# Transposed first hidden columns in a spare accumulator bank, with a semaphore of their own

## The reference, cut to what matters

```python
for i in range(DEPTH_2):
    mix = ...                          # attention of the layer
    h = layer_norm(DEEPNORM_ALPHA * h + mix, ln_mix_g[i], ln_mix_b[i])
    h = layer_norm(DEEPNORM_ALPHA * h + sq_relu_mlp(h, mlp_w_in[i], mlp_w_out[i]),
                   ln_mlp_g[i], ln_mlp_b[i])
```

## Time and profile before

| what | value |
|---|---|
| median of three runs | 1334.9 us (1334.03 to 1336.12) |
| the profiled execution, its own time | 1336.56 us |
| its span, first to last instruction | 1334.8 us |
| mean granted clock of PE, share of full speed | 0.956 |
| PE busy | 1177.5 us, 88% of the span |
| DVE busy | 691.5 us, 52% |
| ACT busy | 490.5 us, 37% |

### The profile page before, as it was taken

One profiled execution on the slowest core, in us unless ns is written; L12 is line 12 of the kernel. 1 busy time (PEld: TensorE's weight loads), 2 busy tenths in 40 slices (PEclk: granted clock), 3 DMA queues, 4 the chain that ended last, 5 costly groups with the idle time before them and its releaser, 6 DMA issues.

```text
span 1334.8 us, 22156 instructions
## 1 busy us (share of the span) xinstructions
PE 1177.5 (88%) x9399; PEld 922.1 (69%) x9399; DVE 691.5 (52%) x1033; ACT 490.5 (37%) x709; POOL 3.9 (0%) x8
## 2 busy tenths in 40 slices
PE   6999999998885767657566999999999999999997
PEld 5688888886542434334233799778888899788886
DVE  4699867774220102011010666765666767766665
ACT  5653446553110100000000554644444456444442
POOL 0000000000000000000000000000000000000000
PEclk9999999999997878888788999999999999999999
DMA  9867487689999999999999955353636245463610
GB/s 358 309 216 261 170 308 268 252 342 406 425 426 426 429 427 427 426 430 428 428 429 415 305 201 190 126 190 130 248 131 247 82 159 218 147 227 134 246 69 32
DMA packets 92743, 369.94 MB, mean 277 GB/s; under 512 B 6654, under 2 KB 14636, under 8 KB 79604
## 3 DMA queue, kind: packets, MB, share of 16 engines
q1 hardware_dynamic: 92280, 367.92, 70.6%
q10 hardware_dynamic: 380, 0.81, 0.2%
HBM read 367.66 MB, written 1.05 MB: 276 GB/s over the span
## 4 chain that ended last, share of the span: by engine, by line
PE 71%; DMA 22%; DVE 3%; ACT 2%; issue 1%; SPq 1%; DVEq 0%; ACTq 0%
DMA arena<-in_moe_w 20%; PE ring L2222 8%; PE ring L2710 6%; PE ring L2211 5%; PE acc L2337 5%; PE acc L2339 5%; PE acc L2338 5%; PE ring L2224 4%; PE ring L2213 3%; DMA own<-in_moe_w 2%; PE acc L2195 2%; PE acc L2196 2%; PE acc L2197 2%; PE ring L2385 1%; PE ring L2387 1%; PE ring L2386 1%
## 5 line engine op out<-in xcount | busy, mean ns | idle before, releaser
L2710 PE MATMUL ring<-arena 128*32 128x256 f32 x1952 | 148.8, 470 | 73.5 <-DMA arena<-in_moe_w 72.5
L2710 PEld LDWEIGHTS ring<-arena 128*32 128x32 f32 x1952 | 76.7, 134 | 141.3 <-issue 76.0
L1430 DVE TENSOR_TENSOR wlo<-arena,whi 128x2048 fp32r<-128x2048 f32 x56 | 128.2, 2290 | 53.7 <-ACT whi L953 53.7
L1880 DVE TENSOR_TENSOR arena<-arena,ring 128x128 f32<-128x128 f32 x32 | 12.2, 380 | 256.0 <-ACT arena L1226 256.0
L1226 ACT ACTIVATE arena<-ring 128x128 f32<-128x128 f32 x32 | 8.9, 277 | 346.2 <-PE ring L2710 342.7
L953 ACT ACTIVATE whi<-arena 128x2048 fp32r<-128x2048 f32 x56 | 107.0, 1910 | 46.3 <-PE acc L2339 29.7
L2222 PE MATMUL ring<-xboth,whi 128*128 128x512 f32 x288 | 102.4, 398 | 0.0
L2224 PE MATMUL ring<-xboth,wlo 128*128 128x256 f32 x288 | 80.8, 281 | 0.0
L2337 PE MATMUL acc<-whi,hidhi 128*128 128x512 f32 x168 | 66.7, 397 | 2.9 <-DVE arena L2131 2.2
L2211 PE MATMUL ring<-hboth,w1hi 128*128 128x512 f32 x192 | 68.0, 399 | 0.1
L2748 PE MATMUL acc<-above 32*128 32x256 f32 x512 | 46.0, 425 | 24.4 <-DVE above L1887 16.6
(11 more groups left out here) (462 smaller groups left out, 2719.0 us busy)
## 6 DMA issues: line engine op xcount, KB each, us to landing
arena<-in_moe_w SPq DMA_DIRECT2D x75, 2048.0 KB, 22.2
arena<-in_mlp_w_in SPq DMA_DIRECT2D x16, 2048.0 KB, 9.7
arena<-in_mlp_w_out SPq DMA_DIRECT2D x16, 2048.0 KB, 8.0
own<-in_moe_w SPq DMA_DIRECT2D x14, 2048.0 KB, 25.7
arena<-in_w_in SPq DMA_DIRECT2D x9, 2048.0 KB, 8.2
arena<-in_w_mod SPq DMA_DIRECT2D x6, 2048.0 KB, 12.9
arena<-in_moe_w SPq DMA_DIRECT2D x11, 1024.0 KB, 13.5
own<-in_w_mod SPq DMA_DIRECT2D x4, 2048.0 KB, 11.1
```

The source lines that it names most:

```text
L1430: dve.tensor_tensor(lo, raw, hi.bitcast(F32), ALU.subtract).then_inc(G["split_ready"], 1)
L2710: ins = pe.matmul(o, xs[:, kt, j, :], w[kt][g], start=(kt == 0), stop=(kt == KT - 1), skip_group_check=bool(early))
```

## The change

The first chunk's four transposes go to the first bank of the second token tile of `acc` (both column blocks side by side, 512 values), and not to two banks of the ring. Its two uses leave the list of ring uses. PE raises a new semaphore `first_turned` once, after the last transpose; ACT waits for it and copies both column blocks in one instruction, and DVE makes both low parts in one instruction and raises `hid_ready`. `hidden_out(0)` waits for `hid_ready`, as all later chunks do. The transposes are ordered by token tile and within it by column block. The piece in 0 counts as finished when its last product is done (`first_product`).

```diff
@@ bank_plan
-        order += [(f"ff{l}", at, "V") for at in ((1, 0), (0, 0), (0, 1), (1, 1))]
-        order += [(f"ff{l}", (i, j), "V") for i in range(2, FF // 256) for j in range(2)]
+        order += [(f"ff{l}", (i, j), "V") for i in range(1, FF // 256) for j in range(2)]
@@ finished
+            if i == 0:
+                return G["first_product"], TT * l + TT
             return bank_full, BANK_AT[f"ff{l}", (i, 1)] + 1
@@ hidden_before
-            return l * (2 * NFF - 1) + max(0, 2 * i - 1)
+            return 2 * (NFF * l + i)
+        def first_rows(j):
+
+            return acc[:, 1, T * j:T * j + T]
@@ scalar engine
-                for j in range(2):
-                    ins = act.activation(hidhi[:, 0, j, :], take(f"ff{l}", (0, j))[:, 0:T], ACT.Copy)
-                ins.then_inc(G["hid_ready"], 1)
+                act.wait_ge(G["first_turned"], l + 1)
+                act.activation(hidhi[:, 0, :, :], acc[:, 1, 0:2 * T].rearrange("p (j t) -> p j t", j=2), ACT.Copy).then_inc(G["hid_ready"], 1)
@@ vector engine
                 dve.wait_ge(G["hid_ready"], hidden_before(l, 0) + 1)
-                for j in range(2):
-                    b = take(f"ff{l}", (0, j))[:, 0:T]
-                    dve.tensor_tensor(hidlo[:, 0, j, :], b, hidhi[:, 0, j, :].bitcast(F32), ALU.subtract).then_inc(freed["V"], 1)
+                b = acc[:, 1, 0:2 * T].rearrange("p (j t) -> p j t", j=2)
+                dve.tensor_tensor(hidlo[:, 0, :, :], b, hidhi[:, 0, :, :].bitcast(F32), ALU.subtract).then_inc(G["hid_ready"], 1)
@@ tensor engine
-                def first_turned(j):
-                    b = bank(f"ff{l}", (0, j))
+                def first_turned():
                     for tt in range(TT):
                         pe.wait_ge(G["first_squared"], TT * l + tt + 1)
-                        ins = pe.transpose(b[:, tt * P:(tt + 1) * P], hsq[:, 0, tt, j * P:(j + 1) * P], ident)
-                    full(ins)
+                        for j in range(2):
+                            ins = pe.transpose(first_rows(j)[:, tt * P:(tt + 1) * P], hsq[:, 0, tt, j * P:(j + 1) * P], ident)
+                    ins.then_inc(G["first_turned"], 1)
@@ hidden_out
-                    if i == 0:
-                        moved(pe, f"ff{l}", (0, 1))
-                    else:
-                        pe.wait_ge(G["hid_ready"], hidden_before(l, i) + 2)
+                    pe.wait_ge(G["hid_ready"], hidden_before(l, i) + 2)
@@ order on the tensor engine
                 second_half(bank(f"ff{l}", (1, 0)), h, 0)
-                for j in range(2):
-                    first_turned(j)
+                first_turned()
                 second_half(bank(f"ff{l}", (1, 1)), h, 1)
```

More of the change, by code:

```diff
@@ L498, in build @@
         a_step = sem("scalar_step")
-        names = "x1_ready part_ready part_high part_low bc_zero ones_ready tmp_ready base_ready ssq_ready lstd_ready centred_sum ht_ready hid_ready hlow_ready hsq_ready first_product first_squared hhi_ready hlo_ready chi_ready clo_ready prehi_ready prelo_ready pre_used kT_done kc_done kT_ready ghi_ready glo_ready yhi_ready ylo_ready mlow_ready gated mixed zhi_ready zlo_ready abs_ready L_ready lr_ones whi_ready split_ready xhi_ready xlo_ready atthi_ready chosen_ready flag_ready pick_ready put_ready dcol_ready dsilu_scaled scol_zero scol_ready square_ready nstd_ready tn_ready mod_ready c_ready exp1_ready lr_part keys_ready cross_ready h_ready ez_ready ostd_ready on_ready z_ready lg_diff rexp_ready comb_ready ssq_half out_stored eps_ready ttok_ready gain_ready s1_ready hidT_ready put_done projected rope_read rot_ready value_ready scored masked max_ready exp_ready turned_done pT_ready weighted_done att_ready share_diff share_exp scaled_ready crossed_done attlo_ready".split()
+        names = "x1_ready part_ready part_high part_low bc_zero ones_ready tmp_ready base_ready ssq_ready lstd_ready centred_sum ht_ready hid_ready hlow_ready hsq_ready first_product first_squared first_turned hhi_ready hlo_ready chi_ready clo_ready prehi_ready prelo_ready pre_used kT_done kc_done kT_ready ghi_ready glo_ready yhi_ready ylo_ready mlow_ready gated mixed zhi_ready zlo_ready abs_ready L_ready lr_ones whi_ready split_ready xhi_ready xlo_ready atthi_ready chosen_ready flag_ready pick_ready put_ready dcol_ready dsilu_scaled scol_zero scol_ready square_ready nstd_ready tn_ready mod_ready c_ready exp1_ready lr_part keys_ready cross_ready h_ready ez_ready ostd_ready on_ready z_ready lg_diff rexp_ready comb_ready ssq_half out_stored eps_ready ttok_ready gain_ready s1_ready hidT_ready put_done projected rope_read rot_ready value_ready scored masked max_ready exp_ready turned_done pT_ready weighted_done att_ready share_diff share_exp scaled_ready crossed_done attlo_ready".split()
         G = {n: sem(n) for n in names}
```

## The result

The changed kernel takes 1328.12 us (median; five of its six runs lie between 1327.54 and 1328.40), the kernel before 1335.04 (six runs). The ratio is 0.9943 with a 95% interval of 0.9930 to 0.9957, so 7 us less, 5.7 to 9.3 by the interval. The sixth run, 1685.34 us at a granted clock of 0.653 where the others have 0.96, is a disturbed one and is left out. The forecast was 1326.7 with a gain of 8.2 us, which this interval does not exclude.

What follows compares the result with a forecast made beforehand. PE was taken to bound the kernel (71% of the chain, loads 22%). Gaps of 4.74 us and slow clock of 3.47 sum to 8.21 us, taking the median from 1334.9 to 1326.7 us, range 1325.4 to 1331.0.

Steps and rivals of the forecast that it cites:

- The wait for the wrong release: PE's wait at out 0 behind DVE's release of chunk 1's banks: 2.36 and 2.38 us by layer, together 4.74.
- The gap causes the slow clock: PE's lower clock over out 0 in both layers comes from the gap ahead of it and goes with it.
- Rival A: The gap goes but out 0's slow clock stays, from the stage before or its transposes: only 4.74 us gained, 1330.2; chance 0.08.
- Its price: Slow clock over out 0's 24 matmuls: 1.72 and 1.75 us by layer, together 3.47, bounds nothing and 3.47.
- The new chain: ACT's merged copy and DVE's merged difference ahead of out 0: low part ready near 876.1, PE due 877.41, cost nothing.
- Rivals B and C: B: another event replaces out 0's wait, 1334.9, chance 0.04. C: accumulator-bank reads held up beside PE's stream, 1338.2, chance 0.03.
- The covers: Time to spare before PE needs later chunks: in 2 has 3.3 us, the tightest left; out 1 has 2.9.
- The loads: Loads bind only in the experts, slices 10 to 22, where the change touches nothing; no later reader waits.
- The range: Median of the changed kernel between 1325.4 and 1331.0 us, the slow side being rival A's 1330.2 with its spread.
- the case without the clock's part: Only the gaps at out 0 go, 4.74 us gained and not 8.21: 1330.2 us.

Runs made afterwards that it cites:

- the gap filled: Kernel before, with nine 512-column matmuls whose result nobody reads put on PE ahead of the wait of out 0: 1333.14 us, ratio 0.9987.
- a short gap: Changed kernel, with out 0 waiting in addition for ACT's second copy of chunk 1: 1329.25 us, ratio 0.9954.
- the long gap: Changed kernel, with out 0 waiting in addition for the low part of chunk 1: 1343.06 us, ratio 1.0055.
- the wait put back: Changed kernel, with out 0 waiting in addition for DVE's release of bank 1,0, as before the change: 1335.63 us, ratio 1.0005.

## Why the prediction was right, and what it mis-sized

**The wait for the wrong release: right.** The gaps went at the place worked out, 4.07 and 4.12 us by layer with the clock included, and putting one count right gives the whole gain.

**The gap causes the slow clock: right in kind.** With the gap filled there was no fall, a short gap has none, the long one has both. Rival A is refuted here: the transposes run as before in the changed kernel and the clock over out 0 is 1.00 in both layers. The Trainium skill (TensorE: Matmul & The Clock Gate, Part 4: PE-mode transpose) says that a transpose does not count as a busy PE in the same way. Read as rival A reads it, as a fall that stays because the transposes stay, the rule does not hold here. Whether the transposes add to what a gap does, no run here shows.

**Its price: mis-sized.** The step was "so I take the gap as the cause, and the fall as gone with it ... together 3.47 us". That was read from one execution in which the fall came twice, and subtracted from the median of runs whose falls were not known. The kernel before falls in some executions not at all (1332.43), in some once, in some twice (1336.56). Of the 6.95 us between the averages of all runs, 4.74 are the gaps, so 2.2 are left where 3.47 were taken. About 0.2 of that is the slower first matmul behind each gap, which needs no fall; the rest is 1.2 falls of 1.6 us in an execution. The medians beside the experiments alone give 1.4 us for the clock. Eight falls behind twelve gaps are 1.3 in an execution, and they agree with it, as far as twelve can say. That accounts for the 1.3 us by which the first medians fell short. The sign of it stood in the prediction itself: the profiled execution was 1.7 us above the median, the price of one fall. The expectation of the filled gap missed by the same step, and that of the long gap by another: it took the price of a fall as fixed.

**The new chain: right.** The copy lasted 0.60 us and the difference 0.69, where 0.55 and 0.68 were taken; the low part came 1.27 us early (1.3 worked out). Rivals B and C had nothing: nothing took the place of the wait, and the reads of `acc` beside PE's stream were not held up.

**The covers: right.** In 2 had 3.3 us to spare, as worked out, and no new wait of PE appeared. The rest of the layer only moved: from in 2 to the second layer's chunk 1 is 263.68 us before and 263.69 after.

**The loads: too broad a reading, without effect.** The prediction says that they bind only in the experts. PE also waits 8.11 us for one at the very start (L2266), where the change touches nothing either.

**The range** held, since it reached to the case without the clock's part.

What stays open is what decides whether a given gap of 2.2 us is followed by the fall, and where it begins. It isn't seen in the work ahead of it: from the first product of chunk 1 to the gap, PE was busy 6.18 or 6.19 of 6.19 us at a clock of 1.00 in executions with two falls, with one and with none. Some runs without a trace (1338.28 and 1337.55 us of the kernel before, 1338.17 with the wait put back) lie over 1 us above the 1336.3 of two falls; the fall in the experts above shows one way in which that can come about, but it was not seen in them.

## What to carry to other kernels

Where releases of several buffers share one counter, a wait for "the n-th of the list" is a wait for n releases in the order in which the engine makes them: compare the two orders, and see whether the late wait is also what guards another buffer. A loss that follows a gap (a slower clock) is to be counted in several executions before it is priced; one profile gives its size, not its frequency. A wide spread over runs of one kernel, beside a narrow one of its neighbour, can be the sign that such a loss comes and goes.

## What the runs showed of the hardware

In the kernel before, a break of PE of 2.2 us was followed by the lower clock (1.2 GHz) behind eight of twelve; with the wait put back, one of 2.35 to 2.37 us behind both. One of 0.47 us was followed by it behind none of two, one of 4.8 us behind both. Where it came, out 0 took 7.0 to 7.2 us after the breaks of 2.2 to 2.4 us, with the clock low from somewhere between the first and the sixth matmul on, and 8.2 to 8.4 after the 4.8 us break, low from the first matmul on. Even without a fall, the 24 matmuls behind a wait took 5.57 to 5.62 us and not 5.47: the second one started 0.34 us after the first and not 0.23, so that a wait cost 0.1 us beside its gap.
